# Attention scores without rotation, from one fp32 product or from three products of hi and lo

## The reference

```python
def block(args):
    i, qn_b, qr_b = args
    s = (jnp.einsum('bqhd,bkhd->bhqk', qn_b, k_nope)
         + jnp.einsum('bqhr,bkr->bhqk', qr_b, k_rope))
    s = s.astype(jnp.float32) * scale
    q_pos = i * Q_BLOCK + jnp.arange(Q_BLOCK)
    mask = key_pos[None, :] <= q_pos[:, None]
    s = jnp.where(mask[None, None], s, -jnp.inf)
    p = jax.nn.softmax(s, axis=-1).astype(v.dtype)
    return jnp.einsum('bhqk,bkhd->bqhd', p, v)
```

## Time and profile before

| | |
|---|---|
| median of three runs | 2351.85 us |
| profiled execution | 2350.33 us, span of the engines 2348.5 us |
| PE busy | 2318.6 us (99%), 13484 matmuls |
| DVE busy | 1659.3 us (71%) |
| ACT busy | 1006.2 us (43%) |
| POOL busy | 845.0 us (36%) |
| granted TensorE clock | 0.997 of full speed |

### The profile page before, as it was taken

One profiled execution on the slowest core, in us unless ns is written; L12 is line 12 of the kernel. 1 busy time (PEld: TensorE's weight loads), 2 busy tenths in 40 slices (PEclk: granted clock), 3 DMA queues, 4 the chain that ended last, 5 costly groups with the idle time before them and its releaser, 6 DMA issues.

```text
span 2348.5 us, 33450 instructions
## 1 busy us (share of the span) xinstructions
PE 2318.6 (99%) x13484; PEld 2017.0 (86%) x13484; DVE 1659.3 (71%) x1658; ACT 1006.2 (43%) x1267; POOL 845.0 (36%) x441
## 2 busy tenths in 40 slices
PE   9999999999999999999999999999999999999998
PEld 7888778888789999989899879899977778799997
DVE  6687588772479687768696769686777743686874
ACT  5324443342355344554353454353443342453443
POOL 1321222121047456348256328355310001474561
PEclk9999999999999999999999999999999999999999
DMA  5221232323323332323332232333321122233322
GB/s 176 72 72 55 72 108 89 100 92 99 103 72 101 115 109 86 99 83 106 103 122 88 90 117 91 108 109 102 96 68 39 46 72 89 90 99 109 116 86 85
DMA packets 220048, 219.25 MB, mean 93 GB/s; under 512 B 10897, under 2 KB 217360, under 8 KB 219920
## 3 DMA queue, kind: packets, MB, share of 16 engines
q1 hardware_dynamic: 218992, 215.27, 28.9%
q10 hardware_dynamic: 928, 2.17, 0.4%
HBM read 213.22 MB, written 2.10 MB: 92 GB/s over the span
## 4 chain that ended last, share of the span: by engine, by line
PE 86%; POOL 5%; DVE 3%; issue 2%; DMA 2%; ACT 2%; SPq 0%; DVEq 0%; ACTq 0%; POOLq 0%
PE bank L1296 19%; PE bank L1298 19%; PE bank L1297 19%; PE bank L1290 7%; PE bank L1292 7%; PE bank L1291 7%; PE bank L1877 2%; PE bank L1924 2%; PE bank L1880 1%; POOL sums L659 1%; POOL raw L660 1%; PE bank L1397 1%; POOL sums L662 1%; DVE wlo L2292 1%; DVE sxlo L2295 1%
## 5 line engine op out<-in xcount | busy, mean ns | idle before, releaser
L1291 PE MATMUL bank<-Xlo,whi 128*128 128x256 f32 x1152 | 321.6, 279 | 0.0
L1292 PE MATMUL bank<-Xhi,whi 128*128 128x256 f32 x1152 | 321.6, 279 | 0.0
L1290 PE MATMUL bank<-Xhi,wlo 128*128 128x256 f32 x1152 | 321.5, 279 | 0.0
L659 POOL TENSOR_TENSOR sums<-raw 128x512 f32<-128x512 f32 x72 | 153.4, 2130 | 426.1 <-DMA raw<-in_ffn_post_wg_dram 164.3
L979 ACT ACTIVATE whi<-raw 128x2048 fp32r<-128x2048 f32 x72 | 138.2, 1920 | 370.1 <-PE bank L1298 227.2
L1296 PE MATMUL bank<-xghi,wlo 128*128 128x512 f32 x624 | 245.8, 394 | 8.2 <-DVE xglo L1958 4.4
L1298 PE MATMUL bank<-xghi,whi 128*128 128x512 f32 x624 | 243.7, 391 | 0.0
L1290 PE MATMUL bank<-Xhi,sxlo 128*128 128x256 f32 x864 | 242.3, 280 | 0.4
L1291 PE MATMUL bank<-Xlo,sxhi 128*128 128x256 f32 x864 | 241.2, 279 | 0.0
L1292 PE MATMUL bank<-Xhi,sxhi 128*128 128x256 f32 x864 | 241.2, 279 | 0.0
L1297 PE MATMUL bank<-xglo,whi 128*128 128x512 f32 x608 | 237.6, 391 | 0.0
(11 more groups left out here) (364 smaller groups left out, 5906.9 us busy)
## 6 DMA issues: line engine op xcount, KB each, us to landing
raw<-in_ffn_w_up_dram SPq DMA_DIRECT2D x22, 1024.0 KB, 5.0
raw<-in_ffn_pre_wg_dram SPq DMA_DIRECT2D x22, 1024.0 KB, 5.3
raw<-in_ffn_pre_wu_dram SPq DMA_DIRECT2D x22, 1024.0 KB, 5.3
raw<-in_ffn_post_wg_dram SPq DMA_DIRECT2D x22, 1024.0 KB, 5.3
raw<-in_ffn_post_wu_dram SPq DMA_DIRECT2D x22, 1024.0 KB, 5.3
raw<-in_ffn_pre_wd_dram SPq DMA_DIRECT2D x24, 768.0 KB, 4.4
raw<-in_ffn_post_wd_dram SPq DMA_DIRECT2D x24, 768.0 KB, 4.4
raw<-in_w_in_dram SPq DMA_DIRECT2D x13, 1024.0 KB, 5.0
```

The source lines that it names most:

```text
L659: nc.gpsimd.tensor_tensor(s1, a21, a22, ALU.add).then_inc(adds_done[h], 1)
L1290: nc.tensor.matmul(bank, wl, x, start=first, stop=False, skip_group_check=True)
L1291: nc.tensor.matmul(bank, w, xl, start=False, stop=False, skip_group_check=True)
L1292: return nc.tensor.matmul(bank, w, x, start=False, stop=last, skip_group_check=True)
```

## The change

The product of QN and KN is made as three products of hi and lo. A copy by ACT makes the hi of each key tile from its bank (`head_key_hi`), and DVE subtracts it from the bank where it copied before. DVE writes the queries to a raw tile; ACT copies that to hi (`head_query_hi`), and DVE subtracts (`query_lo`). The new tiles lie in the unused part of slot 1 of `whi`, `wlo` and `raw`, in the place of `sq`, and in `acc`. PE waits for `query_split` ahead of a head's scores, and SP waits for it ahead of the first load of `w_o`, which overwrites slot 1. `three` is the helper of before: lo by hi, hi by lo, hi by hi.

```diff
--- before.py
+++ after.py
@@ -143,7 +143,10 @@
         wlo = sb("wlo", [P, 2 * UNIT], F32R)
         R = sb("R", [P, T])
         acc = sb("acc", [P, T])
-        sq = sb("sq", [P, 2 * T])
+        squares = ExitStack()
+        sq = sb("sq", [P, 2 * T], F32, squares)
+        squares.close()
+        fourth_hi = sb("fourth_hi", [P, 2 * T], F32R)
         work = sb("work", [P, 6 * T])
         Tt, At, Ut = (work[:, 2 * j * T:2 * (j + 1) * T] for j in range(3))
         cols = sb("cols", [P, NVEC])
@@ -242,8 +245,8 @@
         y1.close()
         at = ExitStack()
         sb("at_gap", [P, 56], F32, at)
-        KN = sb("KN", [P, 4 * T], F32, at)
-        QN = sb("QN", [P, 4 * T], F32, at)
+        KN = sb("KN", [P, 4 * T], F32R, at)
+        QN = sb("QN", [P, 4 * T], F32R, at)
         VV = sb("VV", [P, TC * 512], F32, at)
         QRt = sb("QRt", [P, 2 * T], F32, at)
         Prb = sb("Prb", [P, 10 * P], F32, at)
@@ -258,6 +261,14 @@
 
         QRr = Prb[:, 0:2 * T]
         QRs = work[:, 2 * T:4 * T]
+
+        def spare(t, x):
+            o = UNIT + (x + 1) * T
+            return t[:, o:o + T]
+
+        KNhi = [spare(whi, x) for x in range(3)] + [fourth_hi[:, 0:T]]
+        QNhi = [spare(wlo, x) for x in range(3)] + [fourth_hi[:, T:2 * T]]
+        QNraw = [spare(raw, x) for x in range(3)] + [acc[:, :]]
 
         def probs(h):
             return work[:, 2 * T:2 * T + 10 * P] if h % 2 == 0 else Prb[:, :]
@@ -289,6 +300,9 @@
         rope_part_loaded = sem("rope_part_loaded")
         keys_split = sem("keys_split")
         qrope_turned = sem("qrope_turned")
+        key_hi = sem("key_hi")
+        query_hi_ready = sem("query_hi_ready")
+        query_split = sem("query_split")
         sin_signed = sem("sin_signed")
         raw_ready = [sem("raw_ready0"), sem("raw_ready1")]
         whi_ready = [sem("whi_ready0"), sem("whi_ready1")]
@@ -600,6 +614,7 @@
             with sp.Fori(1, QUARTERS) as q:
                 quarter_weights(q)
             sp.wait_ge(qrope_turned, QUARTERS * 64)
+            sp.wait_ge(query_split, QUARTERS * 4)
             column_blocks("w_o", kp(A["w_o_2"][0]), [8, 8])
             ffn(4)
 
@@ -1205,14 +1220,26 @@
             query_hi(0)
             rope_hi(UB["attn"] + 1, 0, GB["dq"] + 4)
             query_hi(1)
+            def head_key_hi(q, x):
+
+                a.wait_ge(groups_done, q * 14 + (GB["attn"] + x + 1))
+                nc.scalar.activation(KNhi[x], banks[x][:, :], ACT.Copy).then_inc(key_hi, 1)
+
+            def head_query_hi(q, j):
+
+                a.wait_ge(evacuated, q * 14 + (GB["attn"] + 11 + j))
+                nc.scalar.activation(QNhi[j], QNraw[j], ACT.Copy).then_inc(query_hi_ready, 1)
+
+            for x in range(4):
+                head_key_hi(0, x)
             root_of(R[:, :], banks[7][:, :], QR * P, query_sums, 1)
 
             def attend(q):
 
-                if isinstance(q, int):
-                    turn_queries(q)
-                else:
-                    turn_queries(q)
+                turn_queries(q)
+                for j in range(4):
+                    head_query_hi(q, j)
+                if not isinstance(q, int):
                     rope_hi(q * 2 + (UB["attn"] + 3), q + 1, q * 14 + (GB["attn"] + 6))
                     a.wait_ge(groups_done, q * 14 + (GB["attn"] + 14))
                     keys_hi(q * 2 + (UB["attn"] + 2), q + 1, 0, UNIT, 4)
@@ -1240,6 +1267,9 @@
                         nc.scalar.activation(PT[:, 0:4 * P], banks[4][:, 0:4 * P], ACT.Copy).then_inc(turned_act, 1)
                     a.wait_ge(turned_ready, q * 12 + (3 * h + 3))
                     nc.scalar.activation(PT[:, 7 * P:10 * P], banks[6][:, 0:3 * P], ACT.Copy).then_inc(turned_act, 1)
+                    if h > 1 and not isinstance(q, int):
+                        for x in (0, 1) if h == 2 else (2, 3):
+                            head_key_hi(q + 1, x)
                     if h < 2:
                         exps(h + 1, TC - 1)
                     a.wait_ge(out_ready, q * 4 + (h + 1))
@@ -1868,14 +1898,16 @@
                     for i in range(i0, i1):
                         if i == i0:
                             pe.wait_ge(evacuated, q * 14 + (gb + 11 + h))
+                            pe.wait_ge(query_split, q * 4 + (h + 1))
                         if h == 0:
                             if i == 3:
                                 pe.wait_ge(evacuated, q * 14 + (gb + 12))
                         else:
                             pe.wait_ge(exp_ready, q * 16 + (4 * (h - 1) + i + 1))
                         n = (i + 1) * P
-                        nc.tensor.matmul(ring[i][:, 0:n], QN[:, h * T + i * P:h * T + (i + 1) * P],
-                                         KN[:, h * T:h * T + n], start=True, stop=False)
+                        c = slice(i * P, (i + 1) * P)
+                        three(ring[i][:, 0:n], QNhi[h][:, c], tile(QN, h)[:, c], KNhi[h][:, 0:n], tile(KN, h)[:, 0:n],
+                              True, False)
                         r = (h // 2) * T + i * P
                         nc.tensor.matmul(ring[i][:, 0:n], QRt[:, r:r + P], Tt[:, (h % 2) * T:(h % 2) * T + n],
                                          start=False, stop=False)
@@ -2617,7 +2649,9 @@
 
             def take_keys(q, x):
                 v.wait_ge(groups_done, q * 14 + (gb + x + 1))
-                nc.vector.tensor_copy(tile(KN, x), banks[x][:, :]).then_inc(evacuated, 1)
+                v.wait_ge(key_hi, q * 4 + (x + 1))
+                nc.vector.tensor_tensor(tile(KN, x), banks[x][:, :], KNhi[x].bitcast(F32), ALU.subtract
+                                        ).then_inc(evacuated, 1)
 
             for x in range(4):
                 take_keys(0, x)
@@ -2645,8 +2679,14 @@
                                             ).then_inc(qrope_part, 1)
                 take_values(8)
                 take_values(9)
+                def query_lo(j):
+                    v.wait_ge(query_hi_ready, q * 4 + (j + 1))
+                    nc.vector.tensor_tensor(tile(QN, j), QNraw[j], QNhi[j].bitcast(F32), ALU.subtract
+                                            ).then_inc(query_split, 1)
+
                 for j in range(2):
-                    take(10 + j, tile(QN, j))
+                    take(10 + j, QNraw[j])
+                query_lo(0)
                 v.wait_ge(qrope_turned, q * 64 + 64)
                 v.wait_ge(sin_signed, 2)
                 for j in range(2):
@@ -2657,7 +2697,8 @@
                     nc.vector.tensor_tensor(tile(QRt, j), tile(QRt, j), tile(QRs, j), ALU.add
                                             ).then_inc(qrope_ready, 1)
                 for j in range(2):
-                    take(12 + j, tile(QN, 2 + j))
+                    take(12 + j, QNraw[2 + j])
+                query_lo(1)
 
                 def maxes(h, i0=0, i1=TC):
                     for i in range(i0, i1):
@@ -2681,7 +2722,9 @@
                                                 ).then_inc(probs_ready, 1)
 
                 maxes(0)
+                query_lo(2)
                 normalise(0)
+                query_lo(3)
                 for h in range(4):
                     if h < 3:
                         maxes(h + 1, 0, TC - 1 if h < 2 else TC)
```

## The result

Before: 2351.47 us (median of 5 runs, 2350.64 to 2352.72). The changed kernel: **2364.19 us** (median of 5, 2363.15 to 2365.59), a ratio of 1.0053, 95% interval 1.0042 to 1.0064: 12.7 us slower. The forecast was 2363.2 us. The profiled execution took 2365.59 us (span 2363.8) and is the longest of the five, so compared with the profiled 2350.33 it shows 2.5 us more than the medians do.

A forecast was written before the change was run, and what follows sets the result against it. PE was taken to bound the kernel, the other engines keeping up narrowly at each quarter's start. Quarters of 3.8 + 3.7 + 3.7 + 0.2 = +11.4 us on 2350.33 give 2361.7; the median, 1.52 above, gives 2363.2, range 2356.0 to 2368.5.

The forecast's parts named there:

- Start of a quarter, DVE: At each quarter's start `query_lo(0)` stands ahead of the rotated part, so the scores begin 0.60 us later.
- ACT, POOL, and DVE behind it: Head 0: query copies delay `keys_hi` and POOL's lo; `query_lo(2)` waits for POOL; product with the values 4.2 us late.
- three shorter PE waits: Sign expected in the trace after: PE waits shorter than 2 us ahead of head 0's product with the values.
- my own rule: DVE with two SBUF inputs and a POOL instruction reading SBUF exclude each other for a whole instruction; who starts first wins.
- PE's products: Scores without rotation: three fp32r products replace one fp32 product, saving 0.27 us per head, 4.4 over 16 heads.
- rival of slow narrow products: In the scores, the triple of 128 columns costs 0.66 us: +2.9, so 2366.1 us; chance 0.17.
- the 0.24: Alternative price in us of the 128-column triple on PE, from the Trainium skill; would lower the final sum by 0.9.
- First and third quarter: Same chain at head 0 as in the second quarter: +3.8 us in the first, +3.7 in the third.
- rival of the falling clock: PE's clock falls behind its wait for head 0's probabilities: three falls add 4.8 us, 2368.0; chance 0.07.
- Last quarter and the covers: Last quarter, without a POOL instruction: +0.7 less 0.54, +0.2 us; key copies hidden in ACT's waits cost nothing.
- the `w_o` load with no margin: SP's new wait moves the first `w_o` load behind the last quarter's `query_lo(3)`: nil margin, stall at most about 1 us.
- DVE runs through POOL: At head 0 `query_lo(2)` does not wait for POOL: +2.4 us in all, 2354.3; chance 0.11.

The follow-up runs named there:

- pool_late: The changed kernel with one more wait: POOL begins the lo of the next quarter's weights only when `query_lo(3)` is done; 2353.20 us.
- keys_first: The changed kernel with ACT's order alone changed: `rope_hi`, copies of queries 0 and 1, `keys_hi`, copies of queries 2 and 3, then the exponentials; 2358.48 us.
- late_copies: The changed kernel with ACT as in keys_first, but query copies 2 and 3 behind head 0's exponentials, their subtractions later, SP's wait only before slot-1 loads; 2356.84 us.
- late_rotated: late_copies with DVE finishing the first rotated tile (multiply, add) before it begins the second; 2366.01 us.
- before_rotated: The kernel before, with only DVE finishing the first rotated tile before the second, as control for late_rotated; 2351.18 us.
- lo_between: late_rotated with `query_lo(1)` moved between the two rotated tiles and POOL's 4.5-us instruction waiting for the second rotated tile; 2350.25 us.
- one_product: The changed kernel with the score product without rotation made as one fp32 product of the hi tiles, the products with lo left out; 2366.91 us.
- lo_behind: The changed kernel with `query_lo(2)` behind the division of head 0 and not ahead of it; 2362.93 us.
- pool_pieces: The changed kernel with POOL's lo of 2048 columns cut into four instructions of 512 columns; 2362.52 us.

## Why the prediction was right

**Start of a quarter, DVE.** Forecast 0.60 for the score's start; measured 0.71 in the second quarter and 0.69 in the first (2.91 later for the score, 2.22 for the last product of queries). In every kernel with `query_lo(0)` ahead of an unchanged rotation PE waits here, 0.66 to 0.69 us in the second quarter.

**ACT, POOL, and DVE behind it.** This step decides the three quarters that make 11.2 of the 11.4 us, and it holds. Forecast and measured, the latter less 6.69: POOL begins at 1783.73 and 1783.70; `query_lo(2)` begins at 1784.5 and 1784.54, and ends at 1788.80 and 1788.77; the product with the values begins at 1793.15 and 1793.20. Second quarter: +3.7 and +3.74. Of the three shorter PE waits that were to follow ahead of the product with the values, only this quarter has its own (0.71). pool_late shows that POOL's place does it: with the late exponentials and the added subtractions left as they are, 11.0 us go.

**The forecast leaned on one cover.** I ordered the cost by what stood behind POOL's start and did not ask what stood just ahead. In the changed kernel nothing did, and that was luck and no reading of mine; keys_first, late_copies and late_rotated lost 3.3 to 4.3 us a quarter there, by a meeting that my own rule names.

**PE's products.** Forecast with the mask's extra at 128, 256, 384 and 512 columns 0.40, 0.40, 0.565, 0.73; measured 0.38 at 128 (1790.65 to 1791.03, behind a short wait; 0.37 right behind a mask in keys_first), 0.45 (1786.36 to 1786.81), 0.60 (1787.27 to 1787.87), 0.78 (1788.54 to 1789.32). The last three are 0.035 to 0.05 dearer: at 512 columns the first of the three takes 0.32 and the others 0.23, so it pays 0.09 and not 0.05. It pays this behind a turning as behind a mask (1797.33 to 1798.11 is 0.78 too). A mask's step in turn went from 0.06 to 0.03. Per head it comes out as forecast: heads 1 to 2 take 7.73 us (1799.89 to 1807.62) where before took 7.99, -0.26 for -0.27. The rival of slow narrow products is out: 0.36 to 0.38 and not 0.66, and so is the 0.24 that the prediction names beside its own price.

**First and third quarter.** Forecast +3.8 and +3.7, measured +4.50 and +4.34. Here the rival of the falling clock was partly true. The stretches behind the wait in the first quarter:

```profile
1747.00:1748.00 1.00, 1.00 (x5) 0.81 (x4) 0.93 (x6) 0.46 (x2) 0.00 (x0) 0.59 0.95 281
1748.00:1749.00 1.00, 1.00 (x3) 0.47 (x2) 0.97 (x4) 0.79 (x3) 0.00 (x0) 0.50 0.99 278
1749.00:1750.00 1.00, 1.00 (x3) 0.22 (x2) 0.39 (x1) 1.00 (x4) 0.00 (x0) 0.50 1.13 310
1750.00:1751.00 1.00, 1.00 (x4) 0.67 (x3) 0.69 (x1) 0.21 (x1) 0.00 (x0) 0.71 0.94 211
```

The granted clock (third from the right) is at half, 1.2 GHz, for 3.4 us, behind a wait of 2.3; the same in the third quarter from 1846.2, and not in the second. I had weighed the wait against the one of 4.43 us, gave this 0.07 and a price of 1.6 a fall. It came twice of three times, at 0.76 and 0.68 us (the table's lengths, as worked out behind it). A fall costs less than the 1.6 because the wait of 0.71 us for the copy to PT, which the second quarter has, is gone where PE is slow: from the fourth block of head 1 to the product with the values the first quarter takes 3.07 us (1746.97 to 1750.04) and the second 2.56 (1797.33 to 1799.89), its wait included. This is the term that was mis-sized, at nothing in the sum: 1.4 us. Between the medians the change costs 12.7 us where 11.4 were forecast, so these falls would be the whole difference, if the executions without a trace have them as well. The forecast time of 2363.2 stands nearer to the 2364.19 because the kernel before was 0.4 us faster this time than the 2351.85 that it was built on.

**Last quarter and the covers.** The forecast counts the quarter's late start, +0.7 less 0.54. Measured from its first rotated product it is 0.27 shorter, and the late start is already in the third quarter's length. From the attention's end to the program's end nothing was lost (+0.05), and no PE wait of the attention is put down to the keys, so the `w_o` load with no margin and the copies of keys cost nothing that shows.

**The sum.** From the first quarter's first rotated product, 2.94 later by 0.72 of its own: 0.72 + 4.50 + 3.74 + 4.34 - 0.27 = 13.0 us in the profiled execution, for 11.4. The other 2.2 of the 15.3 between the two spans lie ahead of the attention, where both run the same instructions: the clock was at half for 6.8 us more, at 307 and 638 us, in that execution. What makes it so is open. Such stretches are in other profiled kernels too, before_rotated among them, so they are not the change's; medians of several runs are what the verdict rests on. *DVE runs through POOL*, the rival that ends near no difference, gives about the time of the kernel in which POOL does come later: pool_late, 2353.20 for its 2354.3.

## What to carry to other kernels

An operation moved on one engine is charged with where it makes another engine's long instruction land: write down each long POOL instruction's start and end, and what DVE has on both sides of it that reads two tiles in SBUF, or has SBUF as its input and its output. Where the two are close, don't leave the order to chance but let a semaphore make it; a wait on POOL that nobody waits for took back 11.0 of 12.7 us. A saving on the busiest engine counts only from the point where the engine behind it keeps up: of 1.08 us a quarter, at best 0.63 arrived in a quarter of the loop (lo_between, the third), and 0.88 in the last, where POOL has no such instruction.

## What the runs showed of the hardware

- POOL and DVE exclude each other for whole instructions in both directions: a DVE subtraction of 512 columns that began 0.15 us behind POOL lasted 4.92 us, one that began 0.10 ahead lasted 0.69 and stretched POOL's 4.53 to 4.99.
- A division with one SBUF tile as input and SBUF as output waits too: 3.46 us for four (128 to 512 columns) instead of 1.27. The maxima, which read PSUM, do not: in late_copies those of 256 and 384 columns take 0.42 and 0.56 us at 1785.21 and 1785.82, beside POOL's instruction of 1784.29, as long as alone (1797.80 and 1798.35 in the changed kernel).
- Three fp32r products take together 0.36 to 0.38 us at 128 columns, 0.43 to 0.45 at 256, 0.60 at 384 and 0.78 at 512, where the first of the three stands behind an fp32 or a bf16 product. At 128 columns that is about the 0.35 of 256 columns in a stream of like products.
- The length of PE's wait alone does not tell whether the clock falls. Behind waits of 2.3 us it fell in two quarters of three of the changed kernel, behind waits of 2.2 in all three of one_product. In late_rotated it fell behind a wait of 3.34 us and not behind one of 3.35. In lo_behind, with waits of up to 1.45, it fell in none; in pool_pieces, with several of at most 0.9 in a quarter, in two. Nor is it the load on the DMA queues: in the changed kernel's second quarter they are 0.99 busy from 1798 to 1799 us at the full clock, and in its third idle while the clock is at half. What decides stays open. Each fall lasted 3.4 us at half the clock and cost 0.7 to 0.9 us.
